# Local attention of a mixed attention/recurrence layer, run between the chunks of its input projection

## What is computed

```python
def hybrid_swa_rwkv(h, w_in, w_out, sinks, mu, w0, ...):
    z = h @ w_in                                    # 256 x 1024 @ 1024 x 2560
    q, k, v = split_cols(z[..., :SWA_COLS], (SWA_Q_COLS, SWA_KV_COLS, SWA_KV_COLS))
    o_a = swa_sink_attention(q, k, v, sinks, alibi_slopes(SWA_HEADS))
    o_b = rwkv7_time_mix(z[..., SWA_COLS:], mu, w0, ...)
    return concatenate([o_a, o_b]) @ w_out
```

## Time and profile before

| what | value |
|---|---|
| device time, median of 3 runs | 2420.0 us (2416.43 to 2423.4) |
| device time of the profiled execution | 2419.12 us |
| its span in the profile | 2417.3 us |
| mean granted TensorE clock | 0.91 of full |
| PE, DVE, ACT busy | 2123.4, 1626.4, 1004.6 us |
| first stage: last projection matmul ends, first recurrence step starts | 82.1 us, 108.26 us |

### The profile page before, as it was taken

How to read it: one execution, slowest core, us unless ns; L and a number is a source line. 1 busy time by engine, 2 the same in 40 slices (tenths; PEclk the granted TensorE clock), 3 DMA queues, 4 the chain that set the end, 5 groups by cost and what they waited for, 6 DMA issues and landing times.

```text
span 2417.3 us, 35850 instructions
## 1 busy us (share of the span) xinstructions
PE 2123.4 (88%) x14424; PEld 1903.4 (79%) x14424; DVE 1626.4 (67%) x2711; ACT 1004.6 (42%) x1704; POOL 0.2 (0%) x4
## 2 busy tenths in 40 slices
PE   7729769999888899999999878489999999678998
PEld 7619659999865699989999855269998998366998
DVE  4467379884155698878857879668887753276555
ACT  4321045455144555444445633244434333345333
POOL 0000000000000000000000000000000000000000
PEclk9769589999877899999989989789999999779999
DMA  7200038746220387667644410047766652303551
GB/s 296 94 0 2 1 106 298 280 162 234 82 112 1 138 301 275 235 232 278 241 165 157 140 53 1 0 165 274 275 222 249 238 189 84 131 1 111 199 187 70
DMA packets 114852, 379.37 MB, mean 157 GB/s; under 512 B 4992, under 2 KB 5120, under 8 KB 113920
## 3 DMA queue, kind: packets, MB, share of 16 engines
q1 hardware_dynamic: 114688, 377.08, 43.5%
HBM read 376.01 MB, written 1.05 MB: 156 GB/s over the span
## 4 chain that ended last, share of the span: by engine, by line
PE 72%; DVE 20%; ACT 3%; issue 2%; DMA 1%; DVEq 0%; SPq 0%; ACTq 0%
PE psum L878 29%; PE psum L894 14%; PE psum L651 7%; PE psum L704 4%; DVE htok L1859 2%; DVE buf L569 2%; PE psum L645 2%; PE psum L1135 2%; PE psum L2277 1%; PE psum L1488 1%; PE psum L1732 1%; DVE buf L2058 1%; PE psum L498 1%; PE psum L861 1%; DVE buf L2039 1%
## 5 line engine op out<-in xcount | busy, mean ns | idle before, releaser
L878 PEld LDWEIGHTS psum<-buf,buf 128*128 128x128 f32 x6048 | 741.7, 192 | 10.6 <-DVE buf L792 1.4
L878 PE MATMUL psum<-buf,buf 128*128 128x256 f32 x6048 | 745.9, 283 | 0.6 <-DVE buf L792 0.6
L894 PE MATMUL psum<-buf,buf 128*128 128x512 f32 x1584 | 384.2, 391 | 3.4 <-DVE buf L941 3.4
L894 PEld LDWEIGHTS psum<-buf,buf 128*128 128x128 f32 x1584 | 289.1, 188 | 59.7 <-DVE buf L941 5.1
L792 DVE TENSOR_TENSOR buf<-ring,buf 128x1024 fp32r<-128x1024 f32 x264 | 310.8, 1219 | 17.7 <-ACT buf L786 16.6
L786 ACT ACTIVATE buf<-ring 128x1024 fp32r<-128x1024 f32 x264 | 263.1, 1046 | 19.9 <-DMA ring<-in_w_ffn 15.6
L651 PE MATMUL psum<-buf,buf 128*128 128x256 f32 x2064 | 255.0, 284 | 9.0 <-DVE buf L569 9.0
L651 PEld LDWEIGHTS psum<-buf,buf 128*128 128x128 f32 x2064 | 249.3, 192 | 14.5 <-DVE buf L569 14.5
L808 DVE TENSOR_TENSOR buf<-ring,buf 128x1024 fp32r<-128x1024 f32 x132 | 161.5, 1223 | 140.7 <-ACT buf L803 140.5
L569 DVE TENSOR_TENSOR buf<-ring,buf 128x1024 fp32r<-128x1024 f32 x132 | 161.2, 1224 | 117.9 <-ACT buf L563 108.5
L803 ACT ACTIVATE buf<-ring 128x1024 fp32r<-128x1024 f32 x132 | 139.3, 1055 | 191.5 <-PE psum L894 188.9
(11 more groups left out here) (318 smaller groups left out, 2337.7 us busy)
## 6 DMA issues: line engine op xcount, KB each, us to landing
ring<-in_w_ffn SPq DMA_DIRECT2D x88, 1536.0 KB, 6.5
modw<-in_w_mod SPq DMA_DIRECT2D x98, 768.0 KB, 7.0
ring<-in_w_conv SPq DMA_DIRECT2D x44, 1536.0 KB, 6.6
ring<-in_w_ssd_in SPq DMA_DIRECT2D x16, 1536.0 KB, 6.8
ring<-in_w_ns_in SPq DMA_DIRECT2D x9, 1536.0 KB, 7.6
ring<-in_w_hy_in SPq DMA_DIRECT2D x7, 1536.0 KB, 19.0
ring<-in_w_ssd_out SPq DMA_DIRECT2D x5, 1536.0 KB, 6.3
ring<-in_w_cmp SPq DMA_DIRECT2D x4, 1024.0 KB, 4.9
```

Source lines behind the costliest of these rows:

```text
L878: ins = E.matmul(b[:, g * T:(g + 1) * T], w[:, wa, g, k, :], h[:, ha, k, :], start=k + n_ == 0, stop=k == KC - 1 and n_ == 2)
L894: ins = E.matmul(acc[:, t, g * 512:(g + 1) * 512], hr[z][:, ha, t * P:(t + 1) * P], wd[z][:, wa, g * 512:(g + 1) * 512], start=j == 0 and ...
```

## The change

The values' columns go from the end of the weight to behind the keys, so they are chunk 6 (`tokens=(6,)`), and the recurrence's chunks are 7 to 20. The code of `attend` is taken apart into functions for the steps of a unit (`attention`), and `attend` itself calls them as before. The first stage doesn't call `attend` any more: it hands the projection a function `tick`, which the main loop calls at each chunk c. From chunk 8 on, each unit takes three chunks: scores and exponentials at its first, `normalize` at its second, `turn` (transposes) at its third, and `outputs` at the next unit's first. The units use PSUM banks 0 and 1 (scores), 2 and 3 (transposes) and 4 and 5 (outputs); the projection of this stage is left with banks 6 and 7 (`ring_of`). With one pair of banks, scores of unit n+1 now wait for the distance step of unit n.

In all projections, step c now writes the evacuation of chunk c-1 first, then the splits of c+1 and c+2, then `tick`, then the matmuls of chunk c.

```diff
             def main(evac, h_pts, ring_of=(4, 5, 6, 7), tick=None):
...
                 for c in range(first, n):
+                    if c:
+                        freed[(c - 1) % nb] = evac(c - 1, bank(ring_of[(c - 1) % nb]), done[c - 1])
                     prepare(c + 1)
+                    prepare(c + 2)
+                    if tick is not None:
+                        tick(c)
                     s, raw, point_w = made[c]
-                    b = bank(4 + c % 4)
+                    b = bank(ring_of[c % nb])
...
                     else:
                         wp_free[c % 3] = [done[c]]
-                    if c:
-                        freed[(c - 1) % 4] = evac(c - 1, bank(4 + (c - 1) % 4), done[c - 1])
...
-            attend(units, T, projected, H_AT)
+            ready = []
+            scores, exponentials, normalize, turn, outputs, outputs_copy = attention(
+                units, T, ready, R_AT + 12288, W_AT + 24576, R_AT + 37888, nsc=1, turn_bank=2, out_bank=4)
+
+            def tick(c):
+                if c == 7:
+                    ready.append((act.sem, act.n))
+                for n, u in enumerate(units):
+                    at = c - 8 - 3 * n
+                    if at == 0:
+                        scores(n, u)
+                        exponentials(n, u)
+                    elif at == 1:
+                        normalize(n, u)
+                    elif at == 2:
+                        turn(n, u)
+                    elif at == 3:
+                        outputs(u)
+                        outputs_copy(u)
+
+            project(evac, h_pts, (6, 7), tick)
```

## The result

The changed kernel takes 2431.1 us (median of 5 runs, 2430.11 to 2433.65) against 2416.7 us (5 runs of the kernel before on the same chip): ratio 1.0058, 95% interval 1.0046 to 1.0070. It is 0.6% slower. The forecast was 2433 us. Its profiled execution took 2433.65 us with a span of 2431.9 us.

What follows compares the result with a forecast made beforehand. The projection was taken as bound by PE, the attention by the length of its chain. Chain +4.2 us and clock +10.0 us sum to +14.2 on the profiled 2419.1 us: forecast 2433 us, range 2421 to 2441 us.

Steps and rivals of the forecast that it cites:

- All four signs: First stage: four PE waits for L1103, evacuations 14 to 18 us apart, four clock falls to 0.50, recurrence starting near 122 us.
- Splits two ahead: Reordered splits and evacuations in all projections: 0.3 us in the first stage, nothing in the two others; bounds 0 to 1.1.
- The chain and its pauses: First stage: chains of 10.49 and 12.50 us make PE wait at the transposes; 30.0 us come for 25.8, +4.2 at full clock.
- the rounds: Four three-chunk rounds of projection with attention, 62.6 us at full clock where twelve chunks took 34.6: 28.0 us added.
- the rest of the stage: First stage outside the rounds: last unit's outputs 1.1 us, the start 0.3, the last chunk's evacuation 0.6.
- The clock: Half clock on PE behind each round's pause: 2.5 us a round, bounds 0 to 3.8, +10.0 us for four rounds.
- The stretches behind: Everything behind the first stage should be shifted and not changed: nothing taken.
- The first recurrence matmuls: PE L1276 to L1278 behind the attention most likely at half clock again; full clock would give back up to 4.6 us; nothing taken.
- Throughput decides: Rival: PE stays full in the first stage and the other attention work hides beneath it: -15.4, 2404 us; chance 0.08.
- The clock stays full: Rival: the pauses in the first stage are too short for the clock to fall: +4.2, 2423 us; chance 0.14.
- The half clock covers all on the path: Rival: 3.8 us in each round and another 4 for the last outputs and chunk 20: +23, 2442 us; chance 0.13.

Runs made afterwards that it cites:

- experiment 1: Changed kernel with the attention put back behind the projection and four banks, new order of splits and evacuations kept: 2417.72 us, ratio 1.0006 to the kernel before.
- experiment 2: Changed kernel with 22 or 38 extra unread matmuls on PE ahead of each unit's transposes: 2421.37 us, ratio 1.0025 to the kernel before.
- the first pair: Further profiled executions of both kernels, nothing altered: kernel before 2419.28 us, changed kernel 2422.36 us.
- experiment 5: Changed kernel, same instructions reordered: scores, maxima and `normalize` ahead of splits, exponentials, transposes and outputs a chunk later: 2400.88 us, ratio 0.9941 to the kernel before.
- experiment 4: Changed kernel with `normalize` ahead of the split of chunk c+3 on DVE: 2417.1 us, ratio 1.0001 to the kernel before.
- the second pair: Another profiled execution of each kernel, nothing altered: kernel before 2410.94 us, changed kernel 2429.89 us.

## Why the prediction was right, point by point

**The sign, the mechanism, the size.** All four signs that it named stand in the trace, two of them a little off: four waits for L1103, a fall of the clock at each, evacuations over three chunks 15.3 to 18.4 us apart (said: 14 to 18), a late first recurrence step (118.2 where 122 was said). Measured 2431.1, predicted 2433. Sign and mechanism were worked out; that the size is met within 2 us is in part luck, since the first stage lost 4.4 us less than was said, and the rest, for which nothing was said, added about as much.

**Splits two ahead (0.3 us in this stage, nothing elsewhere).** Right within what can be measured: experiment 1 gives +0.06% with no change inside the interval. In the changed kernel chunk 2 waits 0.2 us for the evacuation of chunk 0.

**The chain and its pauses (+4.2 us at full clock).** Right. The chain was 10.20 us for the first unit (10.49 said) and for the first large one 12.55 (12.98 said, with the copy ahead). The pauses were 3.64, 5.01, 2.92 and 4.99 us; about 4 and 5.5 were said. At full clock the rounds take 61.0 us (experiment 2; 62.6 said), and the stage is 3.2 us longer. The rounds were put 1.6 us too high and the rest of the stage 0.6 too low.

**The clock (+10.0 us): the term that was mis-sized.** It measured 6.4 us in the rounds, 1.5 to 1.8 in each and not 2.5. The prediction took the nearest row, where 5.7 us ran at half clock after a pause of 5.42 us. That stretch began at about 89.3, 1.2 us before PE went on, and was 6.8 us long in all. Here the half clock lasted 3.4 us in the first three rounds. Nor does it cost half of its length: the chunk behind the first pause took 4.62 us and the same chunk at full clock 3.11 (experiment 2), 1.5 more, where half of 3.4 would be 1.7. In the fourth round it lasted 6.8 us, but PE stood still for 2.85 us of them, which costs nothing. The bounds of 0 to 3.8 a round held it. From the start of chunk 2 to the end of the stage, the three other profiles of the changed kernel are 8.1, 5.8 and 5.9 us longer than experiment 2, and this one 6.4, so the term itself varies by some 2 us.

**The stretches behind (nothing).** Here two errors met. The sum for the first stage was +14.2 us; it was +9.8. The medians say +14.4, so the forecast of the whole came nearer than its largest term. The 3 to 5 us between (by the profiles and by the medians) are seen only in a part where both kernels do the same, and where one kernel's own executions are 7 to 10 us apart; some 2 us of it lie in the recurrence's two lengths, and whether the changed kernel brings the longer one about was not settled. The first recurrence matmuls, for which nothing was taken, gave back little: the first microsecond of them ran at full clock, as the window shows, and then the clock fell as before. Up to the next ACT_TABLE_LOAD (L1322, now L1355) that is 0.7 to 1.0 us in three profiles, and 2.6 in the first pair.

```profile
120.51:121.50 0.99, 0.99 (x6) 0.99 0.00 0
```

**The rivals.** Throughput decides: refuted for this order of the code, and borne out as a measure of what the idea could give: 2404 us was worked out for it, and experiment 5 measured 2400.88. The Trainium skill's "Perfetto Trace Analysis", section "Optimization Strategy", says that interleaving stretches with different busiest engines may improve performance. The runs agree with it for one order of the steps (0.9941); in another order the same interleaving made the kernel slower (1.0058). The instructions of the attention are the same in both. The clock stays full: this was the state of experiment 2, 2421.37 us where 2423 was said, but it took 120 extra matmuls to have it. The half clock covers all on the path: refuted, 6.4 us and not 19.

## What to carry to other kernels

When a chain of small steps is laid between the chunks of a busy loop, count it with what stands ahead of each step on its in-order queue, and put the step that makes the busiest engine wait so many chunks later that this sum fits; here one chunk later turned +0.6% into −0.4%, and taking two waits for a split out as well gave −0.6%. What a pause of TensorE costs is the pause and the slow work behind it: here two pauses of 1.95 and 1.21 us cost only themselves, and four of 2.92 to 5.01 us another 1.5 to 1.8 us each in one execution, 5.8 to 8.1 us for the four together in the other three. Pauses of 3.3 us (experiment 4) didn't leave the clock full either. Before explaining a difference of a few us in a kernel of 2400, profile both kernels more than once: the untouched part alone moved by 7 to 10 us.

## What was not expected of the hardware

The length of the half clock didn't follow the length of the pause. In the first profile pauses of 3.64, 5.01 and 2.92 us were each followed by 3.4 us at 0.50, the clock fell only 0.2 to 1.2 us after PE had gone on (56.60 for a pause that ended at 55.89, 90.80 for one that ended at 89.63), and a pause of 4.99 us had 6.8 us, which began 2.85 us before its end.

Nor did it repeat from one execution to the next. The four pauses are the same in all four profiles of the changed kernel, within 0.03 us. But when it was timed again, the pause of 3.65 us had a stretch of 6.8 us at 0.50, from 0.8 us before its end, as had both pauses of 5.0 us; in the first and the second pair all four stretches were 3.4 us. Every one of these pauses was met by a fall of the clock, sixteen in all. When it fell, from 2.9 us before the end of the pause to 1.5 us behind it, and for how long changed with the execution.
